# Differential attention: the normalisation multiply of query and key rows 0 to 2 moves from GpSimd to VectorE

## What is computed

```python
def rms_norm(x, g):
    y = x * rsqrt(mean(x * x, axis=-1, keepdims=True) + 1e-6)
    return y * g

def rope(x, pos):                       # d = 64, half = 32
    x1, x2 = x[..., :32], x[..., 32:]
    return concatenate([x1 * cos - x2 * sin, x2 * cos + x1 * sin], axis=-1)

def diff_attention(q, k, v, ...):
    q = rope(rms_norm(q, q_g), pos)     # per head: 2 vectors q, 2 vectors k
    k = rope(rms_norm(k, k_g), pos)
    # blocks of 128 queries; keys of later chunks of 64 are masked
    s = einsum('bhcqd,bhckd->bhcqk', q_blk, k) * scale
    p = softmax(where(allowed, s, -inf))
    a = p[:, :, 0] - lam * p[:, :, 1]
    o = einsum('bhqk,bhkv->bhqv', a, v)
    return rms_norm(o, sub_g) * (1 - lambda_init)
```

## Time and profile before

| | |
|---|---|
| Three runs, us | 2330.93, 2333.91, 2339.49 (median 2333.91) |
| The profiled execution, us | 2330.74 (span of the engines 2328.9) |
| Mean granted clock of TensorE, share of full speed | 0.975 |
| TensorE busy | 2224.8 us, 96% |
| VectorE busy | 1567.8 us, 67% |
| ScalarE busy | 1310.4 us, 56% |
| GpSimd busy | 288.8 us, 12% |

### The profile page before, as it was taken

The page is one execution under the profiler, slowest core; times in us unless marked ns, Lnnn a source line. Parts: engine busy times, 40 slices in busy tenths (PEclk is TensorE's granted clock), DMA queues, the critical chain, the costliest instruction groups (busy, mean ns, idle before and its releaser), DMA issues.

```text
span 2328.9 us, 30235 instructions
## 1 busy us (share of the span) xinstructions
PE 2224.8 (96%) x10196; PEld 1790.4 (77%) x10196; DVE 1567.8 (67%) x1695; ACT 1310.4 (56%) x1534; POOL 288.8 (12%) x383
## 2 busy tenths in 40 slices
PE   5999897999998999999799999999999999999997
PEld 5888675775665888888678888888888888888885
DVE  4777454544433334435689888898898888988984
ACT  5555443334222533323267777777777777777773
POOL 1333100200212000001111101101111011011000
PEclk9999998999999999999699999999999999999998
DMA  4110231311112243334589999999999999999992
GB/s 179 55 54 27 100 109 58 124 61 37 37 45 77 86 136 96 130 99 158 204 312 371 365 365 369 362 366 368 361 369 366 368 365 364 367 375 361 366 363 82
DMA packets 89010, 515.71 MB, mean 221 GB/s; under 512 B 15108, under 2 KB 16132, under 8 KB 38184
## 3 DMA queue, kind: packets, MB, share of 16 engines
q1 hardware_dynamic: 79736, 498.14, 57.5%
q0 software_dynamic: 9216, 16.81, 3.0%
HBM read 508.59 MB, written 23.33 MB: 228 GB/s over the span
## 4 chain that ended last, share of the span: by engine, by line
PE 49%; DVE 1%; ACT 0%; issue 0%; POOL 0%; POOLq 0%; DVEq 0%; ACTq 0%
PE bank L2060 15%; PE bank L2062 15%; PE bank L2061 15%; PE bank L2081 1%; PE bank L2071 1%; PE bank L2112 1%; PE bank L2096 0%; DVE moe_lo L2051 0%; ACT moe_hi L2044 0%; DVE moe_a L2158 0%; DVE moe_um L2152 0%; DVE moe_XTl L2136 0%; POOL out L2210 0%; ACT moe_XTh L2130 0%; DVE moe_aTl L2172 0%
## 5 line engine op out<-in xcount | busy, mean ns | idle before, releaser
L2051 DVE TENSOR_TENSOR moe_lo<-moe_raw,moe_hi 128x2048 fp32r<-128x2048 f32 x382 | 854.8, 2284 | 17.5 <-ACT moe_hi L2044 14.5
L2044 ACT ACTIVATE moe_hi<-moe_raw 128x2048 fp32r<-128x2048 f32 x380 | 728.6, 1920 | 166.4 <-PE bank L2062 159.3
L2060 PE MATMUL bank<-moe_hi,moe_XTh 128*128 128x512 f32 x1024 | 403.8, 394 | 0.0
L2061 PE MATMUL bank<-moe_lo,moe_XTh 128*128 128x512 f32 x1024 | 403.6, 394 | 0.0
L2062 PE MATMUL bank<-moe_hi,moe_XTl 128*128 128x512 f32 x1024 | 403.4, 394 | 0.0
L167 ACT ACTIVATE unit_hi<-unit_raw 128x1024 fp32r<-128x1024 f32 x116 | 122.3, 1059 | 260.2 <-DMA unit_raw<-in_w_units 242.6
L173 DVE TENSOR_TENSOR unit_lo<-unit_raw,unit_hi 128x1024 fp32r<-128x1024 f32 x116 | 142.9, 1237 | 176.6 <-ACT unit_hi L167 174.0
L2062 PEld LDWEIGHTS bank<-moe_hi,moe_XTl 128*128 128x128 f32 x1024 | 193.1, 189 | 44.4
L2061 PEld LDWEIGHTS bank<-moe_lo,moe_XTh 128*128 128x128 f32 x1024 | 193.1, 189 | 44.3
L2060 PEld LDWEIGHTS bank<-moe_hi,moe_XTh 128*128 128x128 f32 x1024 | 193.7, 189 | 40.3
L2060 PE MATMUL bank<-moe_hi,moe_aTh 128*128 128x512 f32 x512 | 200.6, 392 | 1.4 <-DVE moe_aTl L2172 1.4
(11 more groups left out here) (350 smaller groups left out, 3628.3 us busy)
## 6 DMA issues: line engine op xcount, KB each, us to landing
moe_raw<-in_w_moe SPq DMA_DIRECT2D x384, 1024.0 KB, 7.1
unit_raw<-in_w_units SPq DMA_DIRECT2D x116, 512.0 KB, 3.5
da_slab<-in_w_qkv SPq DMA_DIRECT2D x8, 1536.0 KB, 6.8
x_sb<-in_x SPq DMA_DIRECT2D x4, 512.0 KB, 5.0
yda_d<-y_daT SPq DMA_DIRECT2D x1, 2048.0 KB, 6.2
y_daT<-in_blocks_qk SPq DMA_DIRECT2D x1, 2048.0 KB, 8.2
y_daT<-yda_d SPq DMA_DIRECT2D x1, 2048.0 KB, 8.2
y_daT<-in_x SPq DMA_DIRECT2D x1, 2048.0 KB, 8.6
```

The source lines that it names most:

```text
L2044: nc.scalar.activation(HI[ring(n, pos)][:], RAW[pos][:], ACT.Copy).then_inc(s_hi, 1)
L2051: nc.vector.tensor_tensor(LO[pos][:], RAW[pos][:], HI[ring(n, pos)][:].bitcast(F32), ALU.subtract).then_inc(s_lo, 1)
L2060: nc.tensor.matmul(bank[:], xh[:, x], HI[ring][:, w], start=start and k == 0, stop=False)
L2061: nc.tensor.matmul(bank[:], xh[:, x], LO[pos][:, w], start=False, stop=False)
```

## The change

The multiply by `rs` is made by VectorE for all four rows; GpSimd keeps the two instructions that make `rs`. Each of rows 0, 1 and 2 is multiplied at the end of its part of VectorE's body: behind the slab low part for rows 0 and 1, directly behind the rope for row 2. Row 3 stays where it was. A multiply now waits for the power of its own row (`da_qk_rstd`, counted per row). TensorE waits for all four rows on one semaphore. In the prologue the multiply of each row stands behind the slab low part.

```diff
--- before.py
+++ after.py
@@ -291,9 +291,9 @@
     pj, aTb, ob, qkb = K.banks[0:2], K.banks[4], K.banks[5], K.banks[6:8]
     Sb, Sp = [K.banks[2:4], qkb], [K.pairs[1], K.pairs[3]]
     (s_proj, s_pjA, s_pjD, s_ss, s_rope, s_qkT, s_qkTe, s_S, s_nm, s_exp, s_a, s_aT, s_aTe, s_pv, s_oss,
-     s_ors, s_on, s_yT, s_yTe, s_wh, s_wl, s_onr, s_kTe, s_ku, s_rs, s_last) = (K.sem("da_" + n) for n in (
+     s_ors, s_on, s_yT, s_yTe, s_wh, s_wl, s_onr, s_kTe, s_ku, s_rs) = (K.sem("da_" + n) for n in (
          "proj", "proj_used_act", "proj_used_dve", "sumsq", "rotated", "qkT", "qT_kept", "scores",
-         "negmax", "exp", "a", "aT", "aT_kept", "pv", "o_sumsq", "o_rstd", "o_kept", "yT", "yT_kept", "slab_hi", "slab_lo", "o_scaled", "kT_kept", "ca_unit_used", "last_rstd", "last_rotated"))
+         "negmax", "exp", "a", "aT", "aT_kept", "pv", "o_sumsq", "o_rstd", "o_kept", "yT", "yT_kept", "slab_hi", "slab_lo", "o_scaled", "kT_kept", "ca_unit_used", "qk_rstd"))
     FRONT, BACK = range(0, KT // 2), range(KT // 2, KT)
     scale = DH ** -0.5
 
@@ -357,10 +357,7 @@
                     mm.then_inc(s_ku, 1)
 
             def turn_qk(n, i, first=False):
-                if i < TT - 1:
-                    pe.wait_ge(s_rope, n * 3 + (i + 1))
-                else:
-                    pe.wait_ge(s_last, n + 1)
+                pe.wait_ge(s_rope, n * 4 + (i + 1))
                 if not first:
                     pe.wait_ge(s_exp, START + n * 8)
                 for c in range(2):
@@ -545,17 +542,7 @@
 
             def rotate(n, i):
                 hold(K, pool, s_ss, n * 4 + (i + 1))
-                op = rstd(pool, nc, chain, rs[:, i, :], ss[:, i, :], DH, K.half[:, 0:4])
-                if i == TT - 1:
-                    op.then_inc(s_rs, 1)
-                    return
-                chain(op)
-                hold(K, pool, s_pjD, n * 4 + (i + 1))
-                if i == 0:
-                    hold(K, pool, s_qkT, n)
-                nc.gpsimd.tensor_tensor(qk[:, i, :].rearrange("p (g d) -> p g d", g=4),
-                                        t1[:].rearrange("p (g d) -> p g d", g=4),
-                                        rs[:, i, :].unsqueeze(2).broadcast_to([P, 4, DH]), ALU.mult).then_inc(s_rope, 1)
+                rstd(pool, nc, chain, rs[:, i, :], ss[:, i, :], DH, K.half[:, 0:4]).then_inc(s_rs, 1)
 
             def o_rstd(h):
                 hold(K, pool, s_oss, START + h * 4 + 4)
@@ -580,7 +567,7 @@
                 dve.wait_ge(s_pjA, n * 4 + (i + 1))
                 nc.vector.tensor_reduce(ss[:, i, :], sq[:].rearrange("p (g d) -> p g d", g=4), AX,
                                         ALU.add).then_inc(s_ss, 1)
-                dve.wait_ge(s_rope, n * 3 + i)
+                dve.wait_ge(s_rope, n * 4 + i)
                 src = raw[:].rearrange("p (g c d) -> p g c d", g=2, c=2)
                 d1 = t1[:].rearrange("p (g c d) -> p g c d", g=2, c=2)
                 d2 = t2[:].rearrange("p (g c d) -> p g c d", g=2, c=2)
@@ -592,14 +579,14 @@
                                               Sn[:, :, 32:64].unsqueeze(2).broadcast_to([P, 2, 2, 32]), ALU.mult))
                 nc.vector.tensor_tensor(t1[:], t1[:], t2[:], ALU.add).then_inc(s_pjD, 1)
 
-            def rotate_last(n):
-                i = TT - 1
-                dve.wait_ge(s_pjD, n * 4 + 4)
-                dve.wait_ge(s_rs, n + 1)
-                dve.wait_ge(s_qkT, n)
+            def rotate(n, i):
+                dve.wait_ge(s_pjD, n * 4 + (i + 1))
+                dve.wait_ge(s_rs, n * 4 + (i + 1))
+                if i == 0:
+                    dve.wait_ge(s_qkT, n)
                 nc.vector.tensor_tensor(qk[:, i, :].rearrange("p (g d) -> p g d", g=4),
                                         t1[:].rearrange("p (g d) -> p g d", g=4),
-                                        rs[:, i, :].unsqueeze(2).broadcast_to([P, 4, DH]), ALU.mult).then_inc(s_last, 1)
+                                        rs[:, i, :].unsqueeze(2).broadcast_to([P, 4, DH]), ALU.mult).then_inc(s_rope, 1)
 
             def negmax(h, i, wait=True):
                 n, pair = (i + 1) * P, Sp[i % 2]
@@ -646,12 +633,14 @@
                         rope(h + 1, i)
                     if i + 2 < TT:
                         part_lo(h, par, i, more, more2)
+                    if more:
+                        rotate(h + 1, i)
                 weights(h, TT - 1)
                 if more:
                     rope(h + 1, TT - 1)
                 part_lo(h, par, 2, more, more2)
                 if more:
-                    rotate_last(h + 1)
+                    rotate(h + 1, TT - 1)
                 part_lo(h, par, 3, more, more2)
                 if more:
                     keep_kT(h + 1, 1 - par)
@@ -671,7 +660,7 @@
             for i in range(TT):
                 rope(0, i)
                 slab_lo(1, 1, i)
-            rotate_last(0)
+                rotate(0, i)
             keep_kT(0, 0)
             negmax(0, 0, False)
             chain.restart()
```

## The result

| | before | changed |
|---|---|---|
| Median of 13 runs each, us | 2335.98 (2326.77 to 2344.84) | 2346.52 (2341.39 to 2351.88) |
| Ratio, 95% interval | | 1.0037 (1.0021 to 1.0054) |
| The profiled execution, us | 2330.74 | 2348.43 |

The changed kernel is slower by 0.37%, 4.9 to 12.6 us by the interval; the two medians lie 10.5 us apart. The forecast was 11.0 us.

What follows compares the result with a forecast made beforehand. A gapless VectorE-ScalarE line ending in TensorE's wait was taken as the bound: 0.34 + 0.34 + 0.83 = 1.51 us a head, 10.6 over seven, 11.0 with h=0's late power; forecast 2345 us (+0.47%), range 2336 to 2354.

Steps and rivals of the forecast that it cites:

- The line: Unbroken chain through VectorE and ScalarE in each rotating head, ending in TensorE's wait; added multiplies lengthen it 1.51 us a head.
- Rival A: Added multiplies hide in VectorE's idle time or win: 2332 us, 10%.
- rival B: Only the stall in row 2 counts, ScalarE having slack in rows 0 and 1: 6.3 us, 2340 us, 12%.
- Rows 0 and 1: Each multiply stands between a slab low part and the next negmax, delaying it and everything behind by 0.34 us.
- the step "no stall": Row 0 of each following head: the power is done at about 93.2, before the low part ends at 93.62.
- Row 2: VectorE waits about 0.5 us for the power, then multiplies for 0.34, before the weights a(3): 0.83 us more.
- The first head: h=0, first of the seven rotating heads: the 1.51 us of every head, plus 0.46 if row 2's power is late again.
- the late power of the earlier trace: In h=0 row 2's power came after 2.48 instead of 2.02 us; a repeat adds 0.46 us.
- The new wait: TensorE waits about 0.6 us for the weights a(2), before the transposes of row 2 in each head.
- The prologue and the refund: Prologue: 0.34 us into each VectorE gap costs nothing. Refund: rope(3) no longer waits 0.18 us for GpSimd, which buys nothing.
- rival C: TensorE's longer idle lowers its clock: one fall in the stage 2350 us, one in each of seven heads 2381; 8%.
- Behind the stage: After the last head the whole delay stays; no later stage catches up.

Runs made afterwards that it cites:

- the doubled one: The changed kernel with the multiplies of rows 0 and 1 made twice in their places; executed once, 2345.29 us, row 3 transposes 28.01 us apart.
- the run doubled off the line: The changed kernel with all three multiplies behind the next row's weights, those of rows 0 and 1 made twice; executed once, 2338.82 us, distance 25.82 us.
- row 2 alone off the line: The changed kernel with the multiply of row 2 moved behind the weights of row 3; executed once, 2340.90 us, distance 26.48 us.

## Why the prediction was right

**The line.** It was read from waits in both directions: ScalarE waiting for negmax, VectorE for the copies, TensorE for a(3). Undoing its pieces one by one gives 0.85 (row 2) and 0.67 us (rows 0 and 1), 1.52 in all; undoing them together gives 1.48. The pieces add, and two more multiplies a head off the line add nothing to that run. Rival A is refuted by the changed kernel itself, rival B by the run with rows 0 and 1 moved (0.67 where it has 0).

**Rows 0 and 1.** Forecast 0.34 each. In h=2 the first two distances between sums of squares grow from 5.88 to 6.21 and from 6.44 to 6.78 us. In h=1 row 0 grew by 0.51, since the power of row 0 was late (1.19 us from 92.92 on) and the multiply had to stand: the step "no stall" has a margin of only 0.4 us and broke in this head. It did so in every run that has the multiply there (6.39 or 6.40 us in place of 5.88, 6.73 with the doubled one), and in no other head.

**Row 2.** Forecast 0.83, measured 0.93 in the profile: 107.26 - 104.80 = 2.46 against 1.53. The power took the 2.02 us from the sum of squares that it took before. The missing 0.10 is between the end of the power (106.82, by GpSimd's times, which are rough in a profile) and the start of the multiply that waits for it (106.92), which the sum had at zero. Over seven heads that is 0.7 us.

**The first head.** Forecast 1.97, measured 1.15: from its first sum of squares to the end of a(3) 15.85 before (64.48 to 80.33) and 17.00 after (63.95 to 80.95). The late power of the earlier trace rows did not return, and row 2 cost 0.93 there as elsewhere; rows 0 and 1 show 0.06 and 0.16 in place of 0.34 each. For row 1 a slack that the sum did not look for took up the rest: before, VectorE waited 0.18 us for ScalarE's rounded slab part at row 1, after it did not. The 0.06 of row 0 is luck of the two profiles. The same wait at row 0 stands ahead of the multiply, so the multiply can't use it, and yet it is shorter in the changed kernel's profile (the first line is before):

```profile
66.63 0.96 DVE L619 TENSOR_TENSOR da_slab_lo<-da_slab,da_slab_hi 128x768 fp32r<-128x768 f32 x1 [0.53 <-ACT da_slab_hi L501]
```

```profile
65.82 0.96 DVE L606 TENSOR_TENSOR da_slab_lo<-da_slab,da_slab_hi 128x768 fp32r<-128x768 f32 x1 [0.25 <-ACT da_slab_hi L498]
```

It is 0.24 or 0.25 in the four profiles whose first head starts early (see the clock, below), this one among them. Among these, row 0 takes 6.56 us here and 6.21 in the run doubled off the line, which has no multiply there: 0.35. Among those that start late it is 6.86 with the multiply (row 2 alone off the line) and 6.50 without (before): 0.36. So row 0 cost what was forecast, and an estimate for the head at equal start is 0.36 + 0.16 + 0.93 = 1.45, which would make 11.0 for the seven heads.

In the total, seven heads measure 10.7 us (1.15 in h=0, 1.65 in h=1, 1.56 to 1.60 in the others) where 11.0 was forecast. That it comes so near is in part luck: the late power of h=0 stayed away (0.46 less), row 1 of h=0 found a slack (0.18 less) and row 0 of h=0 looks 0.3 too cheap, while the delay behind the power (0.7 more over the seven heads) and the stall in h=1 (0.17 more) were not foreseen.

**The new wait.** TensorE was to wait 0.6 us for a(2); the profile has 0.38 in h=1 and 0.40 in h=2. The weights a(2) are 0.85 us late in h=1 and 0.67 in h=2, and TensorE itself comes 0.47 and 0.27 us later within the head, held up at row 1 (its weight loads idle 0.30 us there in h=1). At row 3 it is 1.58 where 1.5 was forecast.

**The prologue and the refund.** VectorE's gap in the prologue shrank from 1.68 to 1.34 us, and the three multiplies there cost nothing: from the first sum of squares to the fourth it is 12.40 us before and 12.41 after. The 0.18 us for which rope(3) waited are gone and bought nothing: from the row 3 transposes of h=2 to the next sum of squares it is 10.63 before and 10.62 after.

**The clock, rival C.** It is 1.00 over the seven heads with waits of 1.57 to 1.61 us in each. No fall came with waits of that length. The prediction had read it as 1.00 up to 258 us, and that was wrong for the prologue. There TensorE idles 3.11 us for the multiply of row 3 (before 55.07 in the kernel before, 3.12 after) and works at the lower level when it comes back: 0.50 from 56 to 58 us in both profiles. So the falls at the two ends of the stage came with idle times of 3.11 and 2.91 us. How long the lower level holds differs. The stretch before and after:

```profile
51.00:61.00 10.00, 6.89 (x31) 5.66 (x29) 3.98 (x10) 2.15 (x5) 1.32 (x2) 0.66 0.43 157
```

```profile
51.00:61.00 10.00, 6.88 (x38) 6.03 (x38) 4.64 (x13) 2.35 (x6) 1.32 (x2) 0.83 0.43 157
```

From the prologue's last sum of squares to the first of the next head it takes 12.28 us before (52.20 to 64.48) and 11.20 in the changed kernel (52.75 to 63.95), though nothing in the code there differs. Of the ten profiles six have 12.28 or 12.29 and four 11.20 to 11.34, and versions with the same prologue stand on both sides. The 1.1 us belong to the execution, and they flatter the changed kernel in a comparison of the two profiles. One slip in the numbers of C: its price for a single fall, 2350 us, lies within the range of 2336 to 2354 and not above it, so the time alone could not have told C from the forecast; the granted clock does.

**Behind the stage.** No stage behind catches up, as far as the scatter of 2 to 3 us lets one see. The median lies 10.5 us above that of before, by the ratio it is 0.37%, 8.6 us; the interval of 4.9 to 12.6 us is too wide to confirm the sum to better than a few us, and the profiles' distances carry the proof.

## What to carry to other kernels

An engine that is busy two thirds of the time can be on the critical line for most of a head: look where its idle time lies, and whether what ended it was itself waiting for this engine. An added instruction should stand directly in front of such a wait, not behind it; here the same three multiplies cost 1.59 us a head or 0.1 by their place in the stream. Before moving work to a faster engine, ask whether anyone waits for the result: the step on GpSimd took twice as long, and only rope(3) waited for it, 0.18 us a head at a place off the line.

## What was not expected of the hardware

The multiply that waits for GpSimd's power starts 0.10 us after the power's end (106.82 to 106.92), whereas an instruction that follows another on VectorE and does not read its result starts before that one's end: the reciprocal 0.34 us after a multiply that lasts 0.42. A multiply that reads the add in front of it started 0.46 after that one's start. A power of four elements on GpSimd took 1.13 us in the median, 1.01 to 1.19 over the 32 of the stage.

GpSimd's multiply took from 0.61 to 1.30 us for the same 128x256 elements. In the kernel before each of the 24 started while a VectorE instruction with two inputs in SBUF was under way (a slab or unit low part, or the weights), and 23 of them ended 0.46 to 0.48 us after that one's end, whenever they had started; the 24th ended 0.56 after it and took 0.61. VectorE's instructions kept their lengths beside it (the slab low part 948 to 960 ns). In the run that moves only the slab low parts, 14 of the 24 ran beside a reduction with one input instead, and all of these took 0.61 us; the median fell from 824 to 614 ns. So the length of this instruction in a profile goes with what VectorE does beside it. At its shortest it is 1.5 times as long as VectorE's (0.61 against 0.42 us); the factor of two in the prediction is the median beside VectorE's work.

And the same code between 541 and 1067 us of the span took from 525.5 to 535 us in different executions, at a mean granted clock between 0.98 and 0.96; with a spread like that, a change of 4 us is seen in the distances within one stage and hardly in the time.
